# First rankings of a two-layer diffusion trunk taken from unnormalised tokens, on one Trainium2 core

## What is computed

```python
hx2 = modulate(rms_norm(x, norm2[i]), mod_x[3], mod_x[4])      # y * (1 + scale) + shift
x = x + mod_x[5][:, None, :] * peer(hx2, p_w_q[i], p_keys[i], p_u[i], p_v[i])

def peer(h, w_q, sub_keys, u_tab, v_tab):                      # blocks of 128 tokens, 8 heads
        q = (hb @ w_q).reshape(P_BLOCK, P_HEADS, 2, P_DKEY // 2)
        s = jnp.einsum('thpk,hpnk->thpn', q, sub_keys)         # 2 x 128 scores per token and head
        s1, i1 = lax.top_k(s[:, :, 0], P_TOPK)                 # P_TOPK = 16
        s2, i2 = lax.top_k(s[:, :, 1], P_TOPK)
        cand = (s1[..., :, None] + s2[..., None, :]).reshape(P_BLOCK, P_HEADS, P_TOPK * P_TOPK)
        sc, pos = lax.top_k(cand, P_TOPK)
        idx = ...                                              # 16 of 16384 experts
        gate = jax.nn.softmax(sc, axis=-1)
        act = jax.nn.gelu(jnp.einsum('td,thkd->thk', hb, u_tab[idx]), approximate=False)
        return jnp.einsum('thk,thkd->td', gate * act, v_tab[idx])
```

## Time and profile before

| | |
|---|---|
| median of 3 runs | 2463.06 us (2463.0 to 2465.79) |
| the profiled execution | 2467.28 us, of it 2465.5 us span |
| busy of the span: PE, DVE, ACT, POOL | 72%, 66%, 39%, 39% |
| DMA | 938.6 MB, mean 381 GB/s; gathers 807.34 MB |
| granted TensorE clock, mean | 0.857 of full speed |

### The profile page before, as it was taken

How to read it: one execution, slowest core, us unless ns; L and a number is a source line. 1 busy time by engine, 2 the same in 40 slices (tenths; PEclk the granted TensorE clock), 3 DMA queues, 4 the chain that set the end, 5 groups by cost and what they waited for, 6 DMA issues and landing times.

```text
span 2465.5 us, 35630 instructions
## 1 busy us (share of the span) xinstructions
PE 1780.7 (72%) x13118; PEld 850.7 (35%) x13118; DVE 1631.1 (66%) x3826; ACT 972.8 (39%) x2655; POOL 966.9 (39%) x898
## 2 busy tenths in 40 slices
PE   7998988997886769456655666776977855555555
PEld 5877665553552225112221122221633411111111
DVE  1534457968998676577766676775486766666665
ACT  3311136744444333335433353453354433433333
POOL 4014123344444333444444444443043454444442
PEclk9999998999997889778887788887988987867776
DMA  9268769999999999999999999998489999999997
GB/s 354 75 252 333 283 285 388 420 421 420 380 401 423 421 422 391 415 421 421 421 421 421 418 421 420 417 396 349 168 368 421 420 422 420 422 421 421 419 417 297
DMA packets 127967, 938.60 MB, mean 381 GB/s; under 512 B 17168, under 2 KB 18192, under 8 KB 20784
## 3 DMA queue, kind: packets, MB, share of 16 engines
q0 software_dynamic: 114800, 807.34, 79.4%
q1 hardware_dynamic: 12992, 128.97, 13.2%
HBM read 935.10 MB, written 1.15 MB: 380 GB/s over the span
## 4 chain that ended last, share of the span: by engine, by line
DMA 41%; PE 36%; DVE 11%; issue 6%; ACT 5%; POOL 0%; DVEq 0%; SPq 0%; POOLq 0%; ACTq 0%
DMA arena<-in_experts,expert_cur 36%; PE ps L2199 13%; PE ps L1248 12%; DMA last_slot<-in_experts,expert_cur 4%; DVE arena L2281 4%; ACT diag L2092 2%; PE ps L1852 2%; PE ps L1260 2%; PE ps L1273 2%; PE ps L1484 1%; ACT coef L2087 1%; PE ps L1465 1%; ACT acts L2086 1%; PE ps L1890 1%; DVE last_slot L2281 0%
## 5 line engine op out<-in xcount | busy, mean ns | idle before, releaser
L2199 PE MATMUL ps<-arena,diag 64*64 64x512 f32 x5464 | 984.5, 768 | 545.8 <-ACT diag L2092 545.7
L2070 POOL DMA_INDIRECT arena<-in_experts,expert_cur x683 | 793.2, 1161 | 1144.0 <-PE ps L2199 913.6
L2281 DVE CUSTOM_DVE_ANT_0 arena<-arena 128x1024 f32<-128x1024 f32 x683 | 838.9, 1229 | 502.3 <-DMA arena<-in_experts,expert_cur 485.6
L2199 PEld LDWEIGHTS ps<-arena,diag 64*64 64x64 f32 x5464 | 237.6, 158 | 1116.8 <-ACT diag L2092 799.9
L2086 ACT ACTIVATE acts<-dots 128x2 f32<-128x2 f32 (+1 forms) x386 | 78.6, 204 | 990.4 <-DVE dots L2281 979.8
L2092 ACT ACTIVATE diag<-consts,coef 128x128 f32<-128x128 f32 x768 | 266.4, 393 | 12.5
L2199 PE MATMUL ps<-last_slot,diag 64*64 64x512 f32 x680 | 215.6, 763 | 49.6 <-ACT diag L2092 49.5
L2087 ACT ACTIVATE coef<-acts,gate_cur 128x1 f32<-128x1 f32 x768 | 185.1, 288 | 12.6
L1248 PE MATMUL ps<-wring 128*128 128x256 f32 (+2 forms) x568 | 146.1, 409 | 0.0
L2070 POOL DMA_INDIRECT last_slot<-in_experts,expert_cur x85 | 103.8, 1221 | 101.2 <-PE ps L2199 86.3
L2281 DVE CUSTOM_DVE_ANT_0 last_slot<-last_slot,arena 128x1024 f32<-128x1024 f32 x85 | 104.5, 1229 | 57.0 <-DMA last_slot<-in_experts,expert_cur 55.7
(11 more groups left out here) (406 smaller groups left out, 1996.0 us busy)
## 6 DMA issues: line engine op xcount, KB each, us to landing
wring<-in_w_mod SPq DMA_DIRECT2D x18, 2048.0 KB, 10.1
wring<-in_ev_w_in SPq DMA_DIRECT2D x14, 1024.0 KB, 9.2
arena<-in_w_mod SPq DMA_DIRECT2D x6, 2048.0 KB, 10.4
wring<-in_ev_w_in SPq DMA_DIRECT2D x6, 2048.0 KB, 13.8
arena<-in_experts,expert_cur POOLq DMA_INDIRECT x683
wring<-in_w_q SPq DMA_DIRECT2D x5, 2048.0 KB, 12.7
wring<-in_ev_w_out SPq DMA_DIRECT2D x3, 2048.0 KB, 12.8
arena<-in_ev_w_in SPq DMA_DIRECT2D x1, 2048.0 KB, 19.8
```

What stands on the lines that cost most here:

```text
L2070: nc.gpsimd.indirect_dma_start(ring_slot(slot), None, table, bass.IndirectOffsetOnAxis(ap=expert_cur[:, par, k:k + 1], axis=0),).then_inc( ...
L2199: last = nc.tensor.matmul(ps[rows_of(o), sum_bank(G // PH, odd, c), :], diag[rows_of(i), k % RING, rows_of(i)], ring_slot(RING_SLOT[G, k]) ...
L2281: ins = nc.vector.tensor_tensor_reduce(out=ring_slot(slot)[:, 0:D], in0=ring_slot(slot)[:, 0:D], in1=place, scale=1.0, scalar=0.0, op0=ALU ...
```

## The change

Layer 0 and layer 1 each take the queries of the first two heads of their first tile from x itself, before the norm. The norm's factor is one number a token and the scale one number a column, and the shift adds a vector that is the same for all tokens. So x is transposed (`turn_x`), multiplied by gain and scale in the copy, and taken through the query weights (("q0a",), ("q1", 2, 0)); the shift goes through the weights and the keys by itself (`shift_q`, `shift_s`), and where the scores are taken, DVE forms score x factor + shift in one instruction. What was ahead of the ranking for other purposes stands behind it now.

```diff
-PACE = 4
+PACE = 6
...
     if s == 0:
-        g += [("ybT", 0), ("out0", 0, 0), ("out0", 0, 1), ("ybT", 1), ("out0", 1, 0)]
-        g += [("ht", "p0", 0, h) for h in range(2)] + [("out0", 1, 1), ("q0a",)]
-        g += [("ht", "p0", 1, h) for h in range(2)] + [("s0", 0, 0), ("q0b",), ("q0", 0, 2)]
-        for h in range(3, WOVEN_FROM):
-            g += [("q0", 0, h), ("s0", h % 2, (h - 2) // 2)]
+        g += [("ybT", 0), ("out0", 0, 0), ("out0", 0, 1), ("xT", 0), ("shift_q",), ("xT", 1), ("q0a",)]
+        g += [("shift_s",), ("s0", 0, 0), ("ybT", 1), ("out0", 1, 0), ("out0", 1, 1)]
+        g += [("ht", "p0", t, h) for t in range(2) for h in range(2)] + [("q0b",), ("q0", 0, 2)]
...
-WOVEN_FROM = 6
-WOVEN = [[("q0", 0, 6)], [("q0", 0, 7), ("s0", 0, 2)], [("s0", 1, 2), ("s0", 0, 3)], [("s0", 1, 3)]]
+WOVEN = [[("q0", 0, 3)], [("q0", 0, 4), ("s0", 0, 1)], [("q0", 0, 5), ("s0", 1, 0)], [("q0", 0, 6), ("s0", 1, 1)],
+         [("q0", 0, 7), ("s0", 0, 2)], [("s0", 1, 2), ("s0", 0, 3)], [("s0", 1, 3)]]
...
                 take_yb(0)
+                act.wait_ge(p0_column_taken, len(COLUMNS_P0))
+                bank = in_bank(act, ("xT", 0))
+                for k in range(4):
+                    last = A_(raw_xT[:, k, :], bank[:, k * P:(k + 1) * P], ACT.Copy, scale=mod_columns_p0[:, 1, k, 0:1])
...
                 residual(0, 0)
                 residual(0, 1)
+                dve.wait_ge(p0_column_taken, len(COLUMNS_P0))
+                bank = in_bank(dve, ("xT", 1))
+                for j in range(4):
+                    last = V.tensor_scalar(raw_xT[:, 4 + j, :], bank[:, j * P:(j + 1) * P],
+                                           mod_columns_p0[:, 1, 4 + j, 0:1], None, ALU.mult)
+                free_bank(last, ("xT", 1))
                 norm(0)
+                e = ssq_ready.count(("p0", 0)) - 1
+                bank = in_bank(dve, ("s0", 0, 0))
+                taken(dve, ("shift_s",))
+                free_bank(V.scalar_tensor_tensor(out=m["score"][:, 0, 0:2, :], in0=bank.rearrange("p (h n) -> p h n", h=2),
+                                                 scalar=rstd[:, e:e + 1],
+                                                 in1=shift_s.rearrange("p (h n) -> p h n", h=2), op0=ALU.mult, op1=ALU.add),
+                          ("s0", 0, 0))
+                taken(dve, ("s0", 0, 0))
+                rank_steps(RANKS[0], 0, RANK_STEPS)
                 residual(1, 0)
-                norm_take(dve, V.tensor_copy, "p0", 0, 1, 0, m["hT"])
+                rank_steps(RANKS[1], 0, RANK_EARLY)
                 residual(1, 1)
                 norm(1)
-                take_score(0, 0)
-                taken(dve, ("s0", 0, 0))
-                first_ranks_dve(RANKS[0:2])
...
                 from_a(0, 0)
                 from_a(0, 1)
                 turn_b(0)
-                from_a(1, 0)
                 from_b(0, 0)
                 from_b(0, 1)
-                from_a(1, 1)
+                turn_x(0)
+                pe.wait_ge(p0_column_taken, len(COLUMNS_P0))
+                w_q = wq()
+                bank = out_bank(pe, ("shift_q",))
+                for h in range(2):
+                    last = accumulate(bank[:, h:h + 1], [(w_q[:, k, h * P:(h + 1) * P], mod_columns_p0[:, 0, k, 0:1])
+                                                         for k in range(KT)])
...
+        def later_mod_pe(pe, n):
+
+            if n - 2 in COLUMNS_P0:
+                pe.wait_ge(p0_column_taken, n - 1 - COLUMNS_P0[0])
+            mod_pe(pe, n)
+            if n - 1 in COLUMNS_P0:
+                pe.wait_ge(rows_ready, n)
+                nc.tensor.transpose(ps[:, 6 + (n - 1) % 2, P:2 * P], mod_row[(n - 1) % ROWS], const(IDENT)).then_inc(
+                    p0_column_done, 1)
...
                     if n < TOPK:
-                        slot = (0, 1, 2, 3, 4, 5, 7, RING)[n % (NSLOT - 1)]
+                        slot = (1, 2, 3, 5, RING, 0, 4, 7)[n % (NSLOT - 1)]
                     elif late < 0:
-                        slot = (KEYS_SLOT, 0, 1, 2, 3, 4, 5, 7, RING)[(n - TOPK) % NSLOT]
+                        slot = (KEYS_SLOT, 1, 2, 3, 5, RING, 0, 4, 7)[(n - TOPK) % NSLOT]
...
             pool.wait_ge(slot_free, SLOT_LAST[G, k] + 1 + RING)
+            if G == 0 and k == FREE_SLOTS:
+                pool.wait_ge(h_ready.sem, h_ready.count(("p0", 1)))
             if G == 1 and k == 0:
                 pool.wait_ge(product.sem, product.count(("s0", 1, 3)))
+            if G == 4 * PH and k == FREE_SLOTS1:
+                pool.wait_ge(product.sem, product.count(("qrT", 3)))
...
-                norm_take(dve, V.tensor_copy, "p1", 2, 1, 0, hT1)
-                rope_queries(dve, 3)
-                s1_take(dve, V.tensor_copy, 2, 0)
+                e = ssq_ready.count(("p1", 2)) - 1
+                for p in range(2):
+                    taken(dve, ("shift_s1", p))
...
                 s1_taken(dve, 2, 0)
                 rank_steps(RANKS[4 * PH], 0, RANK_STEPS)
+                rope_queries(dve, 3)
                 for p in range(2):
                     for u in pair_of(p):
                         unit_max_dve(dve, u)
```

201 lines of the change are left out of this document (157 added, 44 removed).

## The result

| | before | after |
|---|---|---|
| median | 2463.03 us (2460.1 to 2467.07, 6 runs) | 2484.42 us (2478.54 to 2488.82, 6 runs) |
| ratio, 95% interval | | 1.0087 (1.0073 to 1.0101) |
| profiled execution, span | 2467.28, 2465.5 | 2485.6, 2483.4 |
| granted clock | 0.857 | 0.857 |

A forecast was written before the change was run, and what follows sets the result against it. The prediction took the DMA engines, full during both layers' gathers, as the bound. Layer 0 +1.3, PACE +1 and layer 1 +6.7 gave +9.0 on the profiled 2467.28, so 2476.3, or 2472 against the median; range 2454 to 2479.

The forecast's parts named there:

- the gap: Layer 0 near 395 us: the existing pause in gathers should close because the queue is deep by then, -3 us.
- PACE: Layer 0's context mixer: denser packing, one empty stage in seven, not five; +1 us, bounds -1 to +6.
- layer 1: First gather 2.8 us earlier, but attention scores and load q1_1 later, engines idle 9.4 before the ninth gather: net +6.7.
- Start of layer 0: First gather of layer 0 at 318.4, 12.6 us earlier.
- column transposes: Four transposes and copies at about 190 us put PE and DVE waits there: 0 to 2.8 us, taken as 1.
- Half loads: Layer 0: half loads 0 and 1, 2 MB, move from idle time into the full DMA stretch, +5 us.
- Head 0: Layer 0's first groups: ninth gather 348.7, idle 3.3; groups 1 to 3 cost 1.9; 17th gather waits for s0(1,3), idle 6.7.
- DVE bound by the packing: Rival, layer 0: PACE at +6 or the gap at 395 kept, 2477 to 2480; chance 0.09 with the start rival.
- the rival on the start: Layer 0: first gather gains 9 us, not 12.6, so 3.6 more; chance 0.09 together with the DVE packing rival.
- Taking turns: Rival, layer 1: load shares bandwidth half and half with gathers and takes 7.4 us, sum 2470; chance 0.08.
- The faster rival: Both layers' earlier starts kept in part: layer 0 -7.6, layer 1 -1 to +2.4, together -7, 2456; chance 0.27.

The follow-up runs named there:

- the run that moves nothing else: Kernel before, with half loads 0 and 1 waiting for q0(0,3) so they fall beside the gathers: 1.0023, +5.5 us.
- the late keys: Keys' slot taken ninth in its round, so the 25th gather waits for s0(1,3): on the changed kernel 1.0073; on layer 0's change with PACE 4 1.0015.
- the last pair: Layer 0's change, keys' slot ninth in its round, head 2's queries woven as first of eight stages: PACE 4 1.0005, PACE 6 1.0023.
- the run with the clean load: Changed kernel, with the fifth gather of head 32 waiting until the load of q1_1 has landed: 1.0080, load 4.7 us.

## Why the forecast was wrong

The forecast was 2472, the median is 2484. Three terms of the sum were wrong: the gap (-3), PACE (+1) and layer 1 (+6.7). On the common clock the error can be split without a rest: gather 97 is at +4.0 where the sum had +1.3 (and +4.3 without the credit for the gap), from there to gather 505 come +5.3 where it had +1 (PACE), and from there to the last +9.6 where it had +6.7 (layer 1). That is 18.9 against 9.0.

- **Start of layer 0: right.** Forecast -13.7 on this clock, which leaves out the 1 us for the column transposes ahead of the zero; measured -13.1.
- **Half loads, +5: right.** +5.5 in the run that moves nothing else.
- **Head 0: right.** Forecast on that clock from 288.2: ninth gather 60.5, 17th 92.2; measured 60.7 and 91.6. Transfer time lost at 340 to 350, 350 to 370 and 370 to 390 us is 3.3, 2.2 and 7.4, forecast 3.3, 1.9 and 6.7. The runs with the late keys take 3 to 5 us of the last back.
- **"The gap at 395 should close: -3": failed.** The step took the gap as bound to a time, and the queue behind the 17th gather as deep enough to cover it. It is bound to a stage, the 32 records of the earlier trace rows and the ACT and DVE work around them, and that stage stands behind WOVEN in the order; with seven stages in place of four it came at 402.85. The nine gathers issued to 387.68 are some 22 us of cover, by 2.5 us each, but behind them only two pairs came (393.51 and 401.41) before the one at 413.44. The groups that release them wait for ACT and DVE: PE stood 8.66 us for `diag` ahead of the one at 389.64. Transfer time lost in the gap was 4.8 us before (395 to 410) and is 6.0 after (410 to 430), so it was under-sized at 3 and did not leave the sum: the step is off by 4.2 by this count and by 2.7 at gather 97. No run takes the stage away; that it is bound to the order is read from the traces, where all that have the longer WOVEN lose 3.5 to 6.0 us at 400 to 440, and the four with the old one 0.8 to 2.2.
- **PACE, +1: too small.** From gather 129 to 161 the seven profiles with PACE 4 have 78.5 to 82.9 us, mean 80.8, the eight with PACE 6 82.9 to 86.9, mean 85.3: 4.4 us. From 193 to 505 they are 2.1 shorter (820.8 against 823.0), so some of it is given back; from 97 to 505 the means are 2.8 apart. The runs have 6 (the kernel before), 4.4 (the last pair) and none (layer 0 alone). 2 to 5 us, inside my bounds, not my value. The rest of the +5.3 is of this pair of executions: the one of the kernel before has the least of all fifteen there (1082.7; the others with PACE 4 have 1085.3 to 1088.8). DVE is busy for 171.12 of the 180 us from 600 on, 95% as forecast, and the DMA rate there fell from 400 to 393 GB/s. The rival "DVE bound by the packing" (PACE at +6 or the gap kept, 2477 to 2480) was the nearest to the time and had, with the rival on the start, 0.09; the gap alone is 3 on top of 2472, so 2475, and its 2477 is PACE at +6.
- **Layer 1, +6.7: the mechanism right, its size wrong, 9 to 11.** The load took 9.5 (9.2 forecast) and the run with the clean load shows why. The chain from it to the ninth gather was 12.3 (13.1). The term that was mis-sized is the end of the attention scores: 10.7 late and not 6.8. The path to it was the one forecast: the rotary work on DVE ended 11.1 us behind the start of the ranking, as in the sum, and PE waited 2.38 us for it. But two durations had been taken at full clock. The ranking started 2.3 us later than forecast (0.5 gained and not 2.8), since shift_q1 took 4.59 us and the queries 5.61, where the run of layer 1 alone has 3.63 and 3.74; and the attention scores took 7.6 us and not 6.2, the first four records 3.57 and not 1.95 (granted clock 0.53 from 1802.4 to 1806.0). In the run of layer 1 alone the ranking gained 3.8, the scores took 8.8, and they were late by 8.6. What the sum left out, and what the order shows, is that PE's latent, rotary and nope products and the norm's transposes moved behind the ranking's scores too; they end only 2.4 us ahead of DVE's work, which is why moving the rotary work away won so little.
- **Taking turns: nearer than it seemed.** The rival had 7.4 us for the load; five loads beside gathers took 8.6 to 9.8 (9.5, 9.1, 9.8, 8.6, 9.6). It had 5.0 us for the bytes, and the bytes took 5.1 to 5.9 us in the four kernels that hold no gather back for the load, with 41 to 48% of the engines' time, so the sharing was near one half. What it missed is that the first packet came 3.4 to 3.5 us behind the issue and not 1.0. The Trainium skill, page "DMA: Bandwidth & Descriptors", section "Queues, rings and completion order", has the engines take turns between queues a packet at a time; the shares of this case agree with that once both queues move. Why the first packet waits is shown by no run.
- The faster rival needed the 17th gather before 375; it came at 376.70, which is 379.9 with the zero of the kernel before. Layer 0 and layer 1 sum: forecast +1.3 + 1 + 6.7, measured +9.3 and +9.6 on the common clock. Of the 2.5 that the medians (21.4) have beyond 18.9, the tail behind the last gather has 2.2 in this pair (28.9 against 26.7); in all fifteen executions it is 26.7 to 29.1, whatever the kernel.

Not settled: how PACE's cost splits between the kernels, why the first packet of a load waits longer beside gathers, and whether the four column transposes delay the front; the zero point lies at 279.8 to 288.3 in four executions with the old front (mean 285.0) and at 283.7 to 291.1 in eleven with the new (286.4).

## What to carry to other kernels

A first transfer that starts earlier pays only if the consumers of the first buffers are earlier too: count, for each buffer, the last thing that its reuse waits for, and list everything that moves behind the new first step, on every engine. An idle moment can be tied to a place in the order and not to a time, as here, so don't credit its end to a shift without checking what holds it. Price a chain at both clocks if the rows show both. Where buffers are reused in a fixed order, put the one with the extra wait last in its round.

## What the hardware showed

- A 1 MB load takes 4.7 to 4.9 us by itself (ten executions) and 8.6 to 9.8 beside gathers (five). Both parts of it grow: where no gather is held back, its first packet comes 3.4 to 3.5 us behind the issue and not 1.0, and its bytes take 5.1 to 5.9 us and not 3.6, which is 177 to 205 GB/s.
- In layer 1 of this execution the granted clock was 1.00 until 1778 us, with PE busy all along, then 0.63 to 1781 in the stretch of the 32 one-column records and 0.50 (1.2 GHz) to 1784 in the queries behind them. These took 4.59 and 5.61 us; in the runs of layer 1 alone and in the two that hold gathers back, the same records took 3.63 and 3.74. So the same work on the same path has the lower clock in some executions and not in others. The stretches 1775.8 to 1781.0 and 1781.6 to 1787.3 of the kernel after (clock is the third number from the end):

```profile
1775.80:1781.00 5.20, 5.20 (x38) 5.13 (x37) 1.38 (x2) 1.21 (x5) 0.00 (x0) 0.78 0.00 0
...
1781.60:1787.30 5.70, 5.70 (x36) 5.58 (x35) 3.71 (x7) 2.54 (x6) 0.00 (x0) 0.65 0.00 0
```

In layer 0 the queries behind such records took 5.00 us in this execution (clock 0.73) and 3.74 in that of layer 0 alone (1.00).
- Executions with one and the same front differ by up to 8.5 us before the first gather (288.3 and 279.8 for the same front).
